# The last pair's sums go from PSUM onto the residual, the closing norm moves into the output copies, and the down weights are read in 16 KB runs

## What is computed

```python
def rmsnorm(x, g):
    xf = x.astype(jnp.float32)
    y = xf * lax.rsqrt(jnp.mean(xf * xf, axis=-1, keepdims=True) + NORM_EPS)
    return (y * g.astype(jnp.float32)).astype(x.dtype)

    # in moe_ffn: 32 experts, two per token, hidden width 512, model width 2048
    def expert_block(args):
        xblk, e = args
        return (jax.nn.silu(xblk @ w_gate[e]) * (xblk @ w_up[e])) @ w_down[e]
    yb = lax.map(expert_block, (xb, blk_e)).reshape(n_blk * MOE_BLOCK, d)
    out = jnp.zeros((n, d), jnp.float32).at[st].add(yb[dest].astype(jnp.float32) * sw[:, None])

    # in decoder_layer, and at the end of reference
    x = x + gt2 * ffn
    y_prompt = rmsnorm(hp, norm_f)
    y_sample = rmsnorm(hs, norm_f)
```

## Time and profile before

| | before |
|---|---|
| median of 3 runs | 2600.66 us (2595.79 to 2604.69) |
| the profiled execution | 2600.68 us, span 2598.9 us |
| outside the span | 1.8 us |
| PE busy | 2279.5 us, 88% of the span |
| DVE busy | 730.6 us, 28% |
| ACT busy | 347.0 us, 13% |
| POOL busy | 74.1 us, 3% |
| SP's DMA queue | 642.59 MB, 63.6% of 16 engines' span |
| mean granted TensorE clock | 0.93 of full speed |

### The profile page before, as it was taken

One profiled execution on the slowest core, in us unless ns is written; L12 is line 12 of the kernel. 1 busy time (PEld: TensorE's weight loads), 2 busy tenths in 40 slices (PEclk: granted clock), 3 DMA queues, 4 the chain that ended last, 5 costly groups with the idle time before them and its releaser, 6 DMA issues. The chain is left out here.

```text
span 2598.9 us, 47373 instructions
## 1 busy us (share of the span) xinstructions
PE 2279.5 (88%) x20299; PEld 1625.4 (63%) x20299; DVE 730.6 (28%) x2000; ACT 347.0 (13%) x792; POOL 74.1 (3%) x123
## 2 busy tenths in 40 slices
PE   6899999799999868787677987999998999999996
PEld 4577676677777667655445764665565666655663
DVE  1111211340132145445454124112111122221115
ACT  1001110211210000014322012010100000101001
POOL 0000000000000000001011010000000000000000
PEclk9999999899999977777788998999999999999998
DMA  9887886534344520037669127999999999999990
GB/s 325 341 316 285 315 333 261 147 102 130 106 125 127 129 104 5 4 83 139 202 253 340 65 93 313 425 420 427 417 424 425 421 427 426 420 421 424 422 404 37
DMA packets 205111, 687.54 MB, mean 265 GB/s; under 512 B 38986, under 2 KB 85019, under 8 KB 165371
## 3 DMA queue, kind: packets, MB, share of 16 engines
q1 hardware_dynamic: 195746, 642.59, 63.6%
q0 software_dynamic: 7056, 38.29, 4.7%
q10 hardware_dynamic: 2180, 4.76, 0.5%
HBM read 687.16 MB, written 19.86 MB: 272 GB/s over the span
## 5 line engine op out<-in xcount | busy, mean ns | idle before, releaser
L2766 PE MATMUL bank<-sb_gate_w,sb_x_picked 128*64 128x256 f32 x2048 | 331.8, 389 | 51.6 <-DMA sb_up_w<-in_w_up_dram 51.5
L647 PE MATMUL bank<-sb_hT,sb_sample_kv 128*128 128x296 f32 (+1 forms) x1408 | 355.5, 412 | 12.3 <-PEq L494 12.3
L2766 PE MATMUL bank<-sb_up_w,sb_x_picked 128*64 128x256 f32 x2048 | 330.5, 388 | 0.0
L647 PEld LDWEIGHTS bank<-sb_hT,sb_sample_kv 128*128 128x128 f32 x1408 | 267.9, 191 | 94.7 <-issue 17.5
L2766 PEld LDWEIGHTS bank<-sb_gate_w,sb_x_picked 128*64 128x64 f32 x2048 | 175.8, 140 | 123.4 <-issue 79.2
L2791 PE MATMUL bank<-sb_down_w,sb_hiddenT 128*64 128x512 f32 x1024 | 226.8, 594 | 9.0 <-ACT sb_x_picked L2848 9.0
L469 PE MATMUL bank<-sb_cmp_xT,sb_cmp_w 128*128 128x254 f32 x1024 | 223.3, 379 | 6.6 <-ACT sb_cmp_xT L241 5.8
L469 PEld LDWEIGHTS bank<-sb_cmp_xT,sb_cmp_w 128*128 128x128 f32 x1024 | 193.2, 190 | 38.2 <-ACT sb_cmp_xT L241 8.3
L2766 PEld LDWEIGHTS bank<-sb_up_w,sb_x_picked 128*64 128x64 f32 x2048 | 179.4, 140 | 49.4 <-issue 1.5
L2918 DVE TENSOR_TENSOR sb_hidden<-sb_hidden,bank 128x256 f32<-128x256 f32 x32 | 13.5, 421 | 685.3 <-ACT sb_hidden L2856 685.3
L2791 PEld LDWEIGHTS bank<-sb_down_w,sb_hiddenT 128*64 128x64 f32 x1024 | 84.2, 137 | 128.9 <-issue 115.3
(11 more groups left out here) (567 smaller groups left out, 2283.5 us busy)
## 6 DMA issues: line engine op xcount, KB each, us to landing
sb_gate_w<-in_w_gate_dram SPq DMA_DIRECT2D x64, 2048.0 KB, 14.7
sb_up_w<-in_w_up_dram SPq DMA_DIRECT2D x64, 2048.0 KB, 19.3
sb_down_w<-in_w_down_dram SPq DMA_DIRECT2D x64, 2048.0 KB, 17.7
sb_w_ada<-in_w_ada_dram SPq DMA_DIRECT2D x48, 2048.0 KB, 11.0
sb_sample_kv<-in_w_in_dram SPq DMA_DIRECT2D x22, 2048.0 KB, 8.3
sb_sample_kv<-in_cache_cmp_kv_dram SPq DMA_DIRECT2D x128, 256.0 KB, 7.3
sb_sample_kv<-in_w_out_dram SPq DMA_DIRECT2D x16, 1024.0 KB, 9.8
sb_sample_kv<-in_state_win_kv_dram SPq DMA_DIRECT2D x8, 1024.0 KB, 16.9
```

The lines of the kernel that those rows point to most:

```text
L647: ins = pe.matmul(bank[j % 4][:, 0:wide], ch[:, t, j % 2 * P:(j % 2 + 1) * P], hT[:, t, 0:wide], start=(t == 0), stop=(t == KT - 1))
L2766: ins = pe.matmul(bank[b][64 * half:64 * half + 64, col:col + 256], x[:, t, b * 64:b * 64 + 64], w[i][:, t % CK, half * 256:half * 256 + 256],
```

## The change

1. **Down weights.** The view of `w_down` becomes `(p k)`: partition p holds rows 4p to 4p+3, and each half is one run of 16 KB. The hidden rows must be turned to match: `turn_hidden` is now eight matmuls [64x64] with the identity, each with every fourth column of `h` as the stationary side, in place of two transposes [128x128]. `hiddenT` has the shape [128, 2, 4, 64].
2. **Order in a turn.** `turn_hidden(n, 0)` stands between the two groups of the give matrix's transposes instead of ahead of them.
3. **Last turn.** It is written out behind the loop, with `ahead` false: no `select`, no `index_of`, no gather, no `pick`, no `give_to`. In it DVE adds the gated sum of the pairs 0 to 14 to the residual (`add_gated_acc`), behind its first copy of hidden rows.
4. **Last pair.** DVE reads the steps of `give_back` of pair 15 in PSUM and adds them, gated, right onto `k.xT` (`add_gated_sums`, three instructions for a tile). For each tile ACT then makes the square, and the tile times the norm's weight (into `k.acc`). POOL adds the 16 squares up in `total`.
5. **Norm factor.** PE sums `total` over the features into one column for each token (three matmuls), ACT takes the root of [128, 2] and [32, 1], DVE the reciprocal, and the factor goes in as a scale of the 12 output copies. The reciprocal of [128, 288] and the 16 scalings by it are gone.
6. **Chunks.** They are turned in the order `CHUNKS`, the first three ahead of the sums, over seven banks.
7. **No second phase.** `phase_final` and the meeting of all engines ahead of it are gone. SP issues the output transfers inside `phase_moe`; every engine tests `k.expert` behind its last work.

The core of the diff (left out are names of tiles and semaphores, `begin`, and the parts for the block of extra experts):

```diff
-    d_v = A["w_down"][0, bass.ds(e, 1)].rearrange("o (k p) n -> p (o k) n", p=P)
+    d_v = A["w_down"][0, bass.ds(e, 1)].rearrange("o (p k) n -> p (o k) n", p=P)
...
-        hT = sb("hiddenT", [P, 2, 2, P])
+        hT = sb("hiddenT", [P, 2, 4, SLOTS])
...
+        CHUNKS = ((0, 0), (0, 2), (1, 0), (0, 1), (0, 3), (1, 2), (1, 1), (1, 3), (2, 0), (2, 1), (2, 2), (2, 3))
+        tile_of = lambda i: 8 * (i % 2) + i // 2
+        place_of = lambda m: 2 * (m % 8) + m // 8
+        chunk_bank = lambda c: bank[c % 7]
...
-        def both(eng, turn, last=None):
-            def run(lo, hi):
-                turn(lo, lo == 0, False)
-                with eng.Fori(lo + 1, hi) as n:
-                    turn(n, False, True)
-                if last:
-                    last(hi)
-            run(0, NEXP // 2)
+        def both(eng, begin, turn, last):
+            def run(r, lo, hi):
+                begin(lo)
+                turn(r, lo, lo == 0, False, True)
+                with eng.Fori(lo + 1, hi - 1) as n:
+                    turn(r, n, False, True, True)
+                turn(r, hi - 1, False, True, False)
+                last(r, hi)
+            run(0, 0, NEXP // 2)
             eng.wait_ge(s_extra, 1)
             with eng.If(eng.value_load(k.expert[0:1, N_BLK:N_BLK + 1], min_val=0, max_val=N_OVER) > 0):
-                run(NEXP // 2, N_BLK // 2)
+                run(1, NEXP // 2, N_BLK // 2)
...
+        def copies(eng, copy, parity, r):
+            eng.wait_ge(s_rs, r + 1)
+            for c in range(parity, len(CHUNKS), 2):
+                j, q = CHUNKS[c]
+                n = ROWS[j][1]
+                eng.wait_ge(s_tt, len(CHUNKS) * r + c + 1)
+                copy(k.h2rows[0:n, j, q * 512:(q + 1) * 512], chunk_bank(c)[0:n, :], rstd[0:n, j:j + 1]).then_inc(s_r[parity], 1)
...
+                extras = sp.value_load(k.expert[0:1, N_BLK:N_BLK + 1], min_val=0, max_val=N_OVER)
+                out = (A["y_prompt"][0, 0:P, :], A["y_prompt"][0, P:TP, :], A["y_sample"].rearrange("b t d -> (b t) d"))
+                def results(r):
+                    half = len(CHUNKS) // 2
+                    for j, (_, n) in enumerate(ROWS):
+                        for p in range(2):
+                            done = max(c for c, (i, _) in enumerate(CHUNKS) if i == j and c % 2 == p)
+                            sp.wait_ge(s_r[p], half * r + done // 2 + 1)
+                        sp.dma_start(out[j], k.h2rows[0:n, j, :]).then_inc(s_o, 16)
+                    sp.wait_ge(s_o, 16 * NTT * (r + 1))
+                results(0)
+                sp.wait_ge(k.s_kept, 16)
...
-                    pe.wait_ge(s_h, 2 * n + b + 1)
-                    for cc in range(2):
-                        ins = pe.transpose(bank[2][:, (2 * b + cc) * P:(2 * b + cc + 1) * P], h[:, b, cc * P:(cc + 1) * P],
-                                           k.ident[:, :])
+                    for f in range(4):
+                        for half in range(2):
+                            own = slice(64 * half, 64 * half + 64)
+                            ins = pe.matmul(bank[2][own, (4 * b + f) * SLOTS:(4 * b + f + 1) * SLOTS], h[own, b, f:256:4],
+                                            k.ident[own, own], start=True, stop=True)
                     ins.then_inc(s_ht, 1)
...
-                def turn(n, fresh, before):
+                def turn(r, n, fresh, before, ahead):
                     if not fresh:
                         pe.wait_ge(s_gtc, 2 * n)
                     gate_up(n, 0)
-                    index_of(n + 1)
+                    if ahead:
+                        index_of(n + 1)
                     if before:
                         give_back(n - 1)
-                    turn_hidden(n, 0)
                     pe.wait_ge(s_give, n + 1)
-                    pe.wait_ge(s_ix, 4 * n + 6)
+                    if ahead:
+                        pe.wait_ge(s_ix, 4 * n + 6)
+                    pe.wait_ge(s_h, 2 * n + 1)
                     for b in range(2):
                         for i, (at, r) in enumerate(ROWS):
                             ins = pe.transpose(bank[WB[b]][:, at:at + r], give[0:r, i, b, :, :].rearrange("p a s -> p (a s)"),
                                                k.ident[0:r, 0:r])
                         ins.then_inc(s_gt, 1)
+                        if b == 0:
+                            turn_hidden(n, 0)
                     if not fresh:
                         pe.wait_ge(s_cc, 16 * n)
                     down(n, 0)
                     gate_up(n, 1)
-                    pick(n + 1, False)
+                    if ahead:
+                        pick(n + 1, False)
+                    else:
+                        pe.wait_ge(s_h, 2 * n + 2)
                     turn_hidden(n, 1)
-                    pe.wait_ge(s_xc, 4 * n + 8)
+                    if ahead:
+                        pe.wait_ge(s_xc, 4 * n + 8)
                     down(n, 1)
...
+                def turned(r, hi, c):
+                    j, q = CHUNKS[c]
+                    at, n = ROWS[j]
+                    pe.wait_ge(s_xg, KT * r + 1 + max(place_of(m) for m in range(4 * q, 4 * q + 4)))
+                    if c == 3:
+                        pe.wait_ge(s_cc, 16 * hi)
+                    if c >= 7:
+                        pe.wait_ge(s_r[(c - 7) % 2], len(CHUNKS) // 2 * r + (c - 7) // 2 + 1)
+                    for t in range(4):
+                        ins = pe.transpose(chunk_bank(c)[0:n, t * P:(t + 1) * P], k.acc[:, 4 * q + t, at:at + n], k.ident[:, :])
+                    ins.then_inc(s_tt, 1)
+                def last(r, hi):
+                    give_back(hi - 1)
+                    for c in range(3):
+                        turned(r, hi, c)
+                    pe.wait_ge(s_tot, KT * (r + 1))
+                    for j, (at, n) in enumerate(ROWS):
+                        ins = pe.matmul(bank[7][0:n, j:j + 1], total[:, at:at + n], k.ones[:, 0:1], start=True, stop=True)
+                    ins.then_inc(s_sums, 1)
+                    for c in range(3, len(CHUNKS)):
+                        turned(r, hi, c)
+                both(pe, begin, turn, last)
...
+                def squares_added(r):
+                    for i in range(KT):
+                        pool.wait_ge(s_sq, KT * r + i + 1)
+                        if i == 0:
+                            pool.tensor_copy(total[:, :], sq[:, 0, :]).then_inc(s_tot, 1)
+                        else:
+                            pool.wait_ge(s_tot, KT * r + i)
+                            pool.tensor_tensor(total[:, :], total[:, :], sq[:, i % 4, :], ALU.add).then_inc(s_tot, 1)
                 pool.wait_ge(k.s_h2, 16 * NTT)
                 gather(0, True)
-                for m in range(1, NEXP // 2 + 1):
+                for m in range(1, NEXP // 2):
                     gather(m)
+                squares_added(0)
...
+                def last(r, hi):
+                    act.activation(spare[:, :], k.eps[:, 0:1], ACT.Sqrt)
+                    for i in range(KT):
+                        m = tile_of(i)
+                        act.wait_ge(s_cc, 16 * (hi - 1) + i + 1)
+                        if KT * r + i >= 4:
+                            act.wait_ge(s_tot, KT * r + i - 3)
+                        act.activation(sq[:, i % 4, :], k.xT[:, m, :], ACT.Square).then_inc(s_sq, 1)
+                        act.activation(k.acc[:, m, :], k.xT[:, m, :], ACT.Copy, scale=k.par[:, C_NORMF + m:C_NORMF + m + 1])\
+                           .then_inc(s_xg, 1)
+                    act.wait_ge(s_sums, r + 1)
+                    act.activation(sd[:, 0:2], bank[7][:, 0:2], ACT.Sqrt, bias=k.eps[:, 0:1], scale=1.0 / D)
+                    act.activation(sd[0:NS, 2:3], bank[7][0:NS, 2:3], ACT.Sqrt, bias=k.eps[0:NS, 0:1], scale=1.0 / D).then_inc(s_sd, 1)
+                    copies(act, lambda dst, src, f: act.activation(dst, src, ACT.Copy, scale=f), 0, r)
+                both(act, begin, turn, last)
...
+                def add_gated_sums(n):
+                    by_t = lambda v: v.rearrange("p (b t) -> p b t", t=TS)
+                    dve.wait_ge(s_cc, 16 * n)
+                    for s in range(8):
+                        dve.wait_ge(s_c, 8 * n + s + 1)
+                        for dh in range(2):
+                            m, ps = 8 * dh + s, bank[GB[s % 2][dh]]
+                            dve.tensor_tensor(by_t(part[:, dh, :]), by_t(ps[:, TP:NT]),
+                                              k.mod[:, gate + m, 1:NC].unsqueeze(2).to_broadcast([P, NB, TS]), ALU.mult)\
+                               .then_inc(s_part, 1)
+                            dve.scalar_tensor_tensor(out=k.xT[:, m, 0:TP], in0=ps[:, 0:TP], scalar=k.mod[:, gate + m, 0:1],
+                                                     in1=k.xT[:, m, 0:TP], op0=ALU.mult, op1=ALU.add)
+                            dve.wait_ge(s_part, 16 * (n - (NEXP // 2 - 1)) + 2 * s + dh + 1)
```

(18 more changed lines are left out.)

127 lines of the change are left out of this document (44 added, 83 removed).

## The result

The changed kernel takes **2580.97 us** in the median of 5 runs (2576.19 to 2583.57); the kernel before took 2600.62 beside it (2589.55 to 2604.69). The ratio is 0.9924, 95% interval [0.9904, 0.9944]. It is faster by 20 us, not by the 30.6 forecast, and the median lies above the range of 2561 to 2579. Even the lower end of that interval is a gain of only 29 us, so the forecast of 30.6 was too large in either.

What follows compares the result with a forecast made beforehand. Weight transfers pace the turns, PE's steps the last turn, a serial chain the end. Down weights 6.3, last turn 0.8 and end 23.5 make 30.6 us off 2600.68: 2570 us, range 2561 to 2579.

Steps and rivals of the forecast that it cites:

- The down halves of experts 1 to 29, 58 transfers: Loads between pacing start and last wait for weights: only these 58 transfers were counted as gaining from 16 KB runs.
- 58 x 0.108 = 6.3 us: Down weights in the turns: each transfer 0.108 us shorter at 430 GB/s than at 420.7, 6.3 us off in all.
- the rival of 409 GB/s for the 8 KB runs: Loads in the turns: 8 KB runs move only 409 GB/s, so longer runs bring more; 2561.8 us, chance 0.10.
- "0.8 us" off the last turn: Last turn: earlier `give_back` is offset by the turning, a shorter way to `down` in the second half saves 0.8 us.
- The end, 29.75 us: From the last `give_back` to the end: 17.7 + 1.55 + 10.5 = 29.75 us, 23.5 us less than 53.2.
- The pace of 0.95 us a tile: The end's 16 tiles: POOL's addition taken at 0.95 us a tile, between 0.5 and 1.3, 15.2 us in all.
- The estimate of 0.65 to 0.75 us for the addition: POOL's addition in the end, by the skill's rule: ACT stays slowest at 0.86 us a tile, total 2568.6 us.
- The rival on the shared port: The end: POOL's and DVE's SBUF additions can't run together, 1.3 us a tile, 5.6 us more, 2575.6; chance 0.15.
- 10.5 for (d) and (e): The end behind the norm factor: turning and copying chunks, last transfer's landing, closing, and PE's jump, 10.5 us together.
- In turns 0 to 14 this costs nothing: Turning the hidden rows: PE's 1.3 us more a pair is hidden by 3.6 us of waiting for weights.
- the jump ends ahead of the last landing: The end: PE's 3.8 us jump over the extra experts' block was put at 10.4 us, just behind the last landing.
- PE didn't become the bound: Rival in the loop's `turn_hidden`: small matmuls don't overlap, 8.1 us more a pair, 2631 us; chance 0.03.

Runs made afterwards that it cites:

- after_rows_first: The changed kernel with the first expert's down weights issued only when the first gather has landed; 2571.02 us, 0.9882 of the kernel before.
- before_rows_first: The kernel before, with the first expert's down weights (8 KB runs) held until the first gather has landed; 2591.5 us, 0.9969 of the kernel before.
- after_short_runs: The changed kernel with down weights back in 8 KB runs and two transposes for the hidden rows; 2574.9 us, 0.991 of the kernel before.
- best_kept_busy: The changed kernel with the first expert's down weights held and PE kept busy by unread transposes ahead of the sums; 2567.82 us, 0.9886 of the kernel before.
- after_again: The changed kernel unchanged, measured in a second series; 2573.98 us, 0.9906 of the kernel before.
- best_two_totals: The changed kernel with held down weights, PE kept busy, samples' gated part in PSUM, two alternating POOL totals; 2562.21 us, 0.9853 of the kernel before.

## Why the prediction was wrong

It had the right sign, the right bound in each stretch that it priced, and the right order of the terms. Its gain was 9.3 us too large on the profiled execution, by four steps and 0.4 us ahead of the router.

**"The down halves of experts 1 to 29, 58 transfers": expert 0 was put at nothing, +3.3 us.** The down weights of expert 0 were left out of the sum, since their loads come before the pacing starts. They run beside the stores that the first gather waits for. I counted for the long runs what they give to their own transfer, and never asked who shares the engines with them. The rows for it were in the trace of before: a store of 1 MB that takes 10.8 us to land. Shown by `after_rows_first`, `before_rows_first` and `after_short_runs`. Its size depends on the execution: in the six with long runs beside the stores the gather came 34.6 to 35.2 us behind the router, 2.0 to 2.9 later than the 32.3 to 32.6 with short runs, and the second expert's load 1.5 to 3.3 later than 48.0.

**"58 x 0.108 = 6.3 us" for the runs: 4.4 us, mis-sized.** The stretch from the second expert's load to the last awaited landing shrank from 898.92 to 894.55 us, which is 0.075 us for each of 58 transfers. The reading of 430 GB/s over 12 us was too high for what 16 KB runs give on the mean of the turns; over 720 us the changed kernel, with 16 KB runs only, moves

```profile
1720.00:2440.00 720.00, 690.29 (x5328) 460.05 (x5326) 150.94 (x504) 70.34 (x144) 11.86 (x12) 0.99 1.00 424
```

against 423 with short runs. In the same 12 us, 1874 to 1886, it moves 431. So 12 us don't give the mean of the turns. The stretches of 6 us move with their edges too: of before, 1951 to 1957 us is the 423 of the earlier trace rows, and one us later, still all but free of 16 KB runs, it reads

```profile
1952.00:1958.00 6.00, 5.48 (x52) 4.43 (x54) 0.00 (x0) 0.00 (x0) 0.00 (x0) 1.00 1.03 429
```

The sum was a difference of two such readings, and that it came within 2 us is in part luck. The 424 also rules out the rival of 409 GB/s for the 8 KB runs, which needs 430 for all 16 KB runs.

**"0.8 us" off the last turn: 1.4 us on, in this execution.** `turn_hidden` took 1.17 us for its 16 records where I took 0.9, and 0.3 us were saved where the clock was the same: 49.8 us in `best_kept_busy` against 50.2 before. That part is the mis-sized term. The other 1.7 us are PE's clock. Behind the last wait for weights it was at 0.79 in the changed kernel and at 1.00 before (8 us from 2493 on):

```profile
2493.00:2501.00 8.00, 6.26 (x43) 4.67 (x45) 0.00 (x0) 0.00 (x0) 0.00 (x0) 0.79 1.01 426
```

```profile
2493.00:2501.00 8.00, 5.50 (x52) 4.46 (x54) 0.00 (x0) 0.00 (x0) 0.00 (x0) 1.00 1.02 426
```

Both waited over 2 us. In `before_rows_first` 1.5 us were lost with the old code, and the changed kernel itself took 49.8 us in `after_again`, where the wait was 0.7 us and the clock stayed at 1.00. So this isn't the change's. The length of the wait alone doesn't decide it: behind 2.2 us the clock fell in six kernels and stayed in two. What does stays open; I made no run for it.

**The end, 29.75 us: 31.3.** The pace of 0.95 us a tile was right by luck. I took it from between two bounds, with the row of one input as the nearest; it is 0.80 us for the addition and 0.15 for POOL's wait for its own semaphore. `best_two_totals` removed the second part. The estimate of 0.65 to 0.75 us for the addition, worked out from the Trainium skill, "GPSIMD Engine Reference", section on elementwise cycle accounting, was too low: the addition took 0.80 us, and with its semaphore POOL, and not ACT, was the slowest. The rival on the shared port had its mechanism right (DVE's addition stands for 0.52 us) and its price wrong: POOL's addition takes 797 ns beside it and 794 ns without it, so DVE waits and POOL doesn't. The factor was there 19.6 us behind the last `give_back`, for which I had 19.3; the sums took 1.21 us instead of 0.83 at the lower clock. The rest, "10.5 for (d) and (e)", was 11.7: the last copy came as worked out, but the last transfer took 4.2 us to land and not the 2.9 of the earlier trace rows:

```profile
out_y_sample_dram<-sb_h2rows SPq DMA_DIRECT2D x1, 256.0 KB, 4.2
```

Why is open: it shares the engines with the second transfer of 1 MB, but it did so in the kernel before as well.

What held: "In turns 0 to 14 this costs nothing", for the transfers still pace the turns, and PE's longer path in a pair is hidden; the gated sum of pairs 0 to 14 lies under PE's work; the jump ends ahead of the last landing; PE didn't become the bound.

The misses all had one sign, and the range left out that they might add up. It also took the scatter of the runs as 4 us either way from three of them, where one of the series above shows over twice that.

## What to carry to other kernels

Where a transfer gets longer packets, list every other transfer that runs beside it and who waits for that, from the first load on, not only in the steady part. In front of a small store or gather on the path, hold back loads that nobody needs yet: here it was worth 7.4 us in the changed kernel, more than a third of what the whole change gave, and 3.1 us in the kernel before. An accumulation on POOL that waits for its own semaphore cost the handover each time (0.15 us here); two totals that take turns removed it. Where the last transfers are the limit, a faster engine ahead of them gains little: 2.9 us earlier at the last issue were 0.8 at the end.

## What the runs showed of the hardware that I had not expected

A store of 1 MB landed after 5.6, 10.8 or 13.5 us, by whether the loads of the down weights ran beside it and with what runs.

PE's granted clock fell to 0.5 while PE was busy without a gap, with one-column matmuls for about half of the time, and stayed at 1.0 where it was busy 72% of a stretch behind a piece of 128-column transposes. In these rows the stretch with the higher busy share has the lower clock.

The stages ahead of the router, the same code in all kernels, took 1536 to 1551 us. The two series of the changed kernel have medians 7 us apart, so of total times alone no part of this change under 5 us could have been judged.
